# Second block's experts: token rows gathered as two halves to 128 partitions and turned in four transposes of 128

## The reference, cut to what matters

```python
# hier_moe_2: hf is (512, 1024); expert_idx (512, 2); weights (512, 2)
combine = jnp.sum(jax.nn.one_hot(expert_idx, 32) * weights[..., None], axis=1)
y = jnp.zeros_like(hf)
for e in range(32):
    he = jax.nn.silu(hf @ w_gate[e]) * (hf @ w_up[e])      # (512, 256)
    y = y + combine[:, e:e + 1] * (he @ w_down[e])         # (512, 1024)
```

## Time and profile before

| | us |
|---|---|
| median of 3 runs | 1526.12 |
| lowest and highest | 1524.87, 1528.68 |
| profiled execution: its own time | 1523.58 |
| its span (first to last instruction) | 1521.7 |

### The profile page before, as it was taken

The page is one execution under the profiler, slowest core; times in us unless marked ns, Lnnn a source line. Parts: engine busy times, 40 slices in busy tenths (PEclk is TensorE's granted clock), DMA queues, the critical chain, the costliest instruction groups (busy, mean ns, idle before and its releaser), DMA issues. The chain is left out here.

```text
span 1521.7 us, 20417 instructions
## 1 busy us (share of the span) xinstructions
PE 1296.7 (85%) x7696; PEld 1039.2 (68%) x7696; DVE 702.7 (46%) x1271; ACT 463.3 (30%) x1011; POOL 419.3 (28%) x358
## 2 busy tenths in 40 slices
PE   7997789949999259899999999999798939987882
PEld 6775567749999248789989888788676725544440
DVE  5787772644443556663745627571233341111112
ACT  4542343123232154442242422513323212111110
POOL 5355112111010214213414234134244112332212
PEclk9999889959999669999999999999899959999896
DMA  6300450179994603101213121222121879999994
GB/s 262 111 0 1 154 179 31 56 294 375 380 385 175 205 7 125 56 1 62 89 51 111 56 85 64 105 84 83 42 99 59 337 304 375 383 378 389 395 369 181
DMA packets 65286, 262.34 MB, mean 172 GB/s; under 512 B 8468, under 2 KB 18324, under 8 KB 52384
## 3 DMA queue, kind: packets, MB, share of 16 engines
q1 hardware_dynamic: 54176, 233.73, 41.0%
q0 software_dynamic: 9216, 20.99, 4.1%
q10 hardware_dynamic: 1792, 6.29, 1.2%
HBM read 242.04 MB, written 29.43 MB: 178 GB/s over the span
## 5 line engine op out<-in xcount | busy, mean ns | idle before, releaser
L1702 POOL TENSOR_TENSOR block_w_lo<-block_w,block_w_hi 128x512 fp32r<-128x512 f32 x96 | 130.5, 1361 | 221.2 <-ACT block_w_hi L1680 221.2
L2366 PE MATMUL e_gu<-e_w,e_xT 128*64 128x256 f32 x896 | 113.1, 410 | 22.8 <-DMA e_w<-in_gu 22.0
L240 PE MATMUL dil_bank<-block_w_hi,xT_hi 128*128 128x512 f32 x288 | 116.9, 406 | 4.3 <-PEq L829 4.3
L1680 ACT ACTIVATE block_w_hi<-block_w 128x512 fp32r<-128x512 f32 x96 | 60.7, 633 | 182.9 <-PE dil_bank L242 117.5
L241 PE MATMUL dil_bank<-block_w_lo,xT_hi 128*128 128x512 f32 x288 | 115.0, 399 | 0.0
L242 PE MATMUL dil_bank<-block_w_hi,xT_lo 128*128 128x512 f32 x288 | 114.9, 399 | 0.0
L2366 PEld LDWEIGHTS e_gu<-e_w,e_xT 128*64 128x64 f32 x896 | 67.4, 147 | 60.2 <-DMA e_w<-in_gu 24.5
L240 PEld LDWEIGHTS dil_bank<-block_w_hi,xT_hi 128*128 128x128 f32 x288 | 77.9, 271 | 8.7 <-issue 4.7
L2428 DVE TENSOR_TENSOR e_prod<-e_sg,e_gu 128x128 f32<-128x128 f32 x32 | 9.2, 289 | 156.0 <-ACT e_sg L2459 156.0
L241 PEld LDWEIGHTS dil_bank<-block_w_lo,xT_hi 128*128 128x128 f32 x288 | 78.1, 271 | 4.0
L242 PEld LDWEIGHTS dil_bank<-block_w_hi,xT_lo 128*128 128x128 f32 x288 | 77.8, 270 | 4.2
(11 more groups left out here) (505 smaller groups left out, 3150.5 us busy)
## 6 DMA issues: line engine op xcount, KB each, us to landing
e_w<-in_gu SPq DMA_DIRECT2D x44, 2048.0 KB, 18.1
e_w<-in_dn SPq DMA_DIRECT2D x48, 1024.0 KB, 20.0
block_w<-in_w_dil SPq DMA_DIRECT2D x9, 2048.0 KB, 8.2
block_w<-in_w_out SPq DMA_DIRECT2D x4, 2048.0 KB, 9.2
block_w<-in_w_gates SPq DMA_DIRECT2D x4, 2048.0 KB, 9.0
w_t<-in_w_in_t SPq DMA_DIRECT2D x12, 512.0 KB, 3.5
slot_rows<-blank SPq DMA_DIRECT2D x12, 512.0 KB, 6.7
slot_rows<-e_y ACTq DMA_DIRECT2D x16, 384.0 KB, 8.7
```

The lines of the kernel that those rows point to most:

```text
L240: pe.matmul(out, lhs[0], rhs[0], start=first, stop=False)
L1680: act.activation(wh[:, j % RING, 0:width[i]], k.w[:, slot, c, 0:width[i]], ACT.Copy).then_inc(hi_ready, 1)
L1702: pool.tensor_tensor(wl[:, j % RING, 0:width[i]], k.w[:, (q0 + i) % 2, c, 0:width[i]], wh[:, j % RING, 0:width[i]].bitcast(F32), ALU.subtr ...
L2366: ins = pe.matmul(gubank[t % 2][g * S:(g + 1) * S, 0:2 * FG], xT[t % 2][:, c * S:(c + 1) * S], w1_piece(slot.of[t], w, 2 * FG), start=(c = ...
```

## The change

`r_xg` is now 128 partitions by 512 in the second block. Partition p holds the first half of slot p's row, partition 64 + p its second half. The view `parts` sees `token_rows` as 1024 rows of 512 numbers, and `r_tok_of` grows to 128 partitions and holds twice the token plus 0 or 1. The new constant `row_half` (2048, or 2049 from partition 64 on) gives that in one DVE operation. A full 128 by 128 transpose of chunk c then turns features 128c to 128c + 127 of all slots, and, from the other partitions, features 512 + 128c on: four transposes in place of eight. `turned_at` says where a chunk now lies in `e_xbank` and `e_xT`. The first block's experts (96 slots) keep `GROUPS` = 1 and their whole rows.

```diff
-          ("half_row", 1), ("upto", 128), ...
+          ("half_row", 1), ("row_half", 1), ("upto", 128), ...
+    c["row_half"] = 2 * NO_TOKEN + k[:, None] // S2
...
-    k.tok_of = k.sb(ctx, f"{name}_tok_of", [S, NT], U32)
+    GROUPS = 2 if 2 * S == P else 1
+    k.tok_of = k.sb(ctx, f"{name}_tok_of", [GROUPS * S, NT], U32)
+    parts = rows.rearrange("t (m f) -> (t m) f", m=GROUPS)
+    k.xg = [k.sb(ctx, f"{name}_xg{i}", [GROUPS * S, DM // GROUPS]) for i in range(2)]
...
-    k.xg = [k.sb(ctx, f"{name}_xg{i}", [S, DM]) for i in range(2)]
...
-                    pool.indirect_dma_start(k.xg[b][:], None, rows, bass.IndirectOffsetOnAxis(
-                        ap=k.tok_of[:, b:b + 1], axis=0), bounds_check=SEQ - 1, oob_is_err=False).then_inc(x_in[b], 16)
+                    pool.indirect_dma_start(k.xg[b][:], None, parts, bass.IndirectOffsetOnAxis(
+                        ap=k.tok_of[:, b:b + 1], axis=0), bounds_check=GROUPS * SEQ - 1, oob_is_err=False).then_inc(x_in[b], 16)
...
-                dve.tensor_scalar(k.tok_of[:], tbank[0:S, 0:NT], float(NO_TOKEN), None, ALU.add).then_inc(tok_ready, 1)
+                if GROUPS == 1:
+                    ins = dve.tensor_scalar(k.tok_of[:], tbank[0:S, 0:NT], float(NO_TOKEN), None, ALU.add)
+                else:
+                    ins = dve.tensor_scalar(k.tok_of[:], tbank[:, 0:NT], float(GROUPS), k.c("row_half"), ALU.mult, ALU.add)
+                ins.then_inc(tok_ready, 1)
...
+        parts = rows.rearrange("t (m f) -> (t m) f", m=GROUPS)
+        PER = KD // GROUPS
+
+        def turned_at(c):
+            return (c % PER * GROUPS + c // PER) * S
...
-                    for c in range(KD):
-                        ins = pe.transpose(xbank[c * 2 // KD][:, c * S % XH:c * S % XH + S],
-                                           xg[t % 2][:, c * P:(c + 1) * P], k.c("ident")[0:S, 0:S])
+                    for c in range(PER):
+                        at = turned_at(c)
+                        ins = pe.transpose(xbank[at // XH][:, at % XH:at % XH + U], xg[t % 2][:, c * P:(c + 1) * P],
+                                           k.c("ident"))
...
-                            ins = pe.matmul(gubank[t % 2][g * S:(g + 1) * S, 0:2 * FG], xT[t % 2][:, c * S:(c + 1) * S],
+                            ins = pe.matmul(gubank[t % 2][g * S:(g + 1) * S, 0:2 * FG], xT[t % 2][:, turned_at(c):turned_at(c) + S],
                                             w1_piece(slot.of[t], w, 2 * FG), start=(c == 0), stop=(c == KD - 1))
```

More of the change, by code:

```diff
@@ L74 @@
 CONSTS = [("ident", 128), ("before", 128), ("ones", 128), ("iota", 128), ("down", 128), ("tok", TT), ("freq", 16),
-          ("half_row", 1), ("upto", 128), ("after", 128), ("rot", 128), ("cos", SEQ), ("sin", SEQ)]
+          ("half_row", 1), ("row_half", 1), ("upto", 128), ("after", 128), ("rot", 128), ("cos", SEQ), ("sin", SEQ)]
 CONST_AT = {}
@@ L2326, in tile @@
                         pool.wait_ge(x_turned, t - 1)
-                        pool.indirect_dma_start(xg[t % 2][:], None, rows, bass.IndirectOffsetOnAxis(
-                            ap=k.tok_of[:, t:t + 1], axis=0), bounds_check=SEQ - 1, oob_is_err=False).then_inc(
+                        pool.indirect_dma_start(xg[t % 2][:], None, parts, bass.IndirectOffsetOnAxis(
+                            ap=k.tok_of[:, t:t + 1], axis=0), bounds_check=GROUPS * SEQ - 1, oob_is_err=False).then_inc(
                                 x_in[t % 2], 16)
```

## The result

The changed kernel took 1508.41 us (median of 1505.68, 1506.26 and 1510.56), the kernel before beside it 1525.89 us. The ratio is 0.9876, with a 95% interval of 0.9855 to 0.9896: **17.5 us, 1.2%, faster**. A fourth run of the changed kernel took 2619.2 us, in a slow state that no other run showed, and is left out. The prediction had 1526.0 us, a range from 1522.0 to 1529.5, and a chance of 0.04 for this side.

What follows compares the result with a forecast made beforehand. The prediction took the second block's expert stage to be DMA-bound. Its terms, 0.05 + 0.12 + 0 + 0 - 0.22 + 0, summed to -0.05 us, giving 1526.0 us for the median, range 1522.0 to 1529.5.

Steps and rivals of the forecast that it cites:

- What bounds the kernel: Second block's experts: DMA engines stay busy and set the stage's end; loads from 1333 us on wait in their queue.
- DMA time of the stream: Second block's stream: gathers hold the engines about 11.6 us and half rows are no dearer; 0 us, range -3.6 to +3.6.
- the good end: Gathers in the stream: if 257 GB/s is the price of 64 partitions, 30 gathers fall from 15.2 to 11.6 us, -3.6 us.
- spreading over 128 partitions helps: Faster rival: first landings gain 2.5 us and the stream's gathers 3.6 us, together -6.1 us, 1519.9 us; chance 0.04.
- Token numbers: Stage's start: the operation on 128 partitions takes 0.25 us instead of 0.20 on 64; +0.05 us on the path.
- Issues of gathers: POOL at the stage's start: 1014 ns per gather instead of 953, two on the path; +0.12 us.
- Packets: First two gathers: two half rows share a packet, so 80 packets per gather and 160 for two, as before.
- half rows cost more: Slower rival: reading 2 KB pieces at half the present rate makes gathers take 23.2 us, not 11.6; 1537.6 us; chance 0.05.
- First landings: First two gathers, before the drain where the engines meet: landing unchanged, 0 us, range -2.5 to +2.5.
- Turn of tile 0: PE at the stage's start, clock 0.50: four transposes of 128 take 1.11 us, eight of 64 took 1.10; 0 us.
- Turn at full clock: PE, tiles 1 and 2: four transposes take 0.60 us instead of 0.71, -0.22 us on the path; other 29 turns hidden.
- Later landings: Gathers issued two tiles ahead, 9.8 us before need: landing stays as it is and PE does not wait; 0 us.

Runs made afterwards that it cites:

- the padded kernel: Kernel before with second-block gathers over 128 partitions, indices of partitions 64 to 127 out of bounds, whole rows on the same 64 partitions: 1517.7 us, ratio 0.9944.
- after_again: The changed kernel itself, unchanged, in a later comparison: 1508.51 us (6 runs) against 1525.65 us for the kernel before, ratio 0.989.

## Why the prediction was wrong

What bounds the kernel: **right**. The DMA engines are the bound from 1333 us on. That is why a change of the rate came through in full: 16.4 us from the stream's first regular load to its last landing, 17.9 us in the span.

The step that failed is **"DMA time of the stream"**. I asked how many microseconds the gathers hold the engines, 11.6, took the good end as 257 GB/s turned into 337, and got at most 3.6 us. Two things were wrong in it. First, the term held only q0's own packets. It took q1's 387 GB/s as a constant, though the question of the change was what a transfer does to the loads beside it. q0's own part was 2.4 us for gathers and scatters together, within the bounds; q1's was 14.2 us, and had no term at all. Second, the row was there. The earlier trace rows shows 257 GB/s while 64-partition gathers moved their rows, and I put it down to "the end of other loads". That reading was wrong: in this microsecond (1244:1245, first fence) q1 had 7.3% of the engines' time. In the same one of the changed kernel (second fence) the first gathers moved their rows at 0.21 / 0.579 = 363 GB/s.

```profile
q1 hardware_dynamic: 16, 0.02, 7.3%
```

```profile
q0 software_dynamic: 121, 0.21, 57.9%
```

The right use of the row would have been to look at the same moment in the dense part. The windows of 1 us above have it in the trace of before: 303 to 365 GB/s when a gather's rows move, 393 to 475 between. A shortfall of some 100 GB/s over 2 to 3 us is 0.2 to 0.3 MB, at 420 GB/s 0.5 to 0.7 us of stream per gather, and 30 gathers make 14 to 21 us. That estimate could have been made blind.

The same view would have given a ceiling: a DMA share of 1.01 is busy time, not speed. Between gathers the same queues moved up to 475 GB/s; the mean of 387 left something to be found.

The rival **"spreading over 128 partitions helps"** had the direction, at 1519.9 us and 0.04. Its mechanism was sized by the same wrong term.

The Trainium skill, "SBUF — State Buffer", section "Can I just issue two DMAs to hit both halves?", says that the ports of the on-chip memory that a transfer uses go by its own span of partitions, and that only one transfer over all 128 reaches all 16. The cut gather agrees with it in its time: two gathers over 64, one to each half, gave 1528.56 us where one over 128 gave 1508.51 us. I had instead weighed what the Trainium skill, "DMA: Bandwidth & Descriptors", section "Rules for kernel authors", says of tile shapes, that 128 partitions mean more and smaller descriptors, and had taken it to speak against the change; 1728 further packets of skipped rows did not raise q0's share (9.9%). The price falls on q1's loads above all, as their packets show. The Trainium skill, "DMA: Bandwidth & Descriptors", section "The descriptor swizzle", gives for 128 partitions which engine writes which partitions, the first eight engines the lower 64. The late end of the padded kernel (1481.45 us, share down to 0.31) fits rows on eight engines only. That 64-partition rows are written by engines whose loads go elsewhere, through ports that others' loads need, is my reading of all this. It fits the scatter, which reads on-chip memory and hinders nothing, and it is argued, not shown: no run separated the port from other consequences of the dealing, and the traces name neither a packet's engine nor its port. What is shown ends at the instruction: over 64 partitions it makes the loads' packets beside it longer, over 128 it does not.

The other steps. Token numbers: 0.27 us, expected 0.25. Issues of gathers: 1.07 and 1.01 us, expected 1.01 each. Packets: two gathers make 160 packets and 0.24 MB, as predicted, so "half rows cost more" fell as expected. First landings: the drain ended 1.1 us earlier, within -2.5 to +2.5 us. Turn of tile 0: 1.11 us, as predicted. Turn at full clock: 0.66 us in the timeline at 1253.51 against 0.71, and the chain's tile is 6.33 us long (1258.40 to 1264.73) instead of the 6.27 predicted: 0.05 us gained a tile, not 0.11, since the price came from a group of four transposes elsewhere. Not in the sum was that gate and up of tile 0 ran 0.77 us shorter. The mean granted clock of that stretch was 0.74 (1248.6 to 1253.6) instead of 0.63 (1249.7 to 1255.4): both begin at the lower level (0.50, 1.2 GHz), and it rose sooner. That is an accident of the execution and no effect of the change: in another profile of the changed kernel (after_again) the same products took 6.16 us, and the first regular load went out at 1254.49. Later landings: 8.0 us in the median and 9.2 at most for the stage's 30 gathers, and no wait for `r_xg` on the chain: right.

## What to carry over

When a kernel is bound by a stream of transfers, read its GB/s in windows of a microsecond, not only its DMA share: a share of 1.0 at 315 GB/s beside 475 a few microseconds later is a transfer that is being hindered, and a small one beside it may be the reason. Price an edit of a transfer by what it does to the queue that carries the bytes, not by its own packets alone. In a stage like this one, let an indirect gather that runs beside large loads be one instruction over 128 partitions with its rows spread over all of them, by halving the rows or even by skipped indices; where TensorE was the bound, in the first block, it brought nothing (1510.58 us).

## What was new of the hardware

- A gather of 64 partitions costs the loads of another queue more than it takes itself: 30 gathers whose own packets hold the engines for an estimated 11.6 us cost the kernel 27 to 30 us. Over 128 partitions the cost is 12 to 13 us (all known to some 7 us). In a stage with the first kind 30.1% of the loads' 16 KB packets took over 650 ns, with the second 0.7%.
- Two gathers over 64 partitions to the two halves of the memory are no substitute for one over 128: 1528.56 against 1508.51 us.
- The direction matters: the scatter, from on-chip memory to HBM, cut the same way cost nothing measurable (1509.8 us).
- Skipped rows took no measurable time of the engines: 5888 packets instead of 4160 on q0 at a share of 9.9 against 10.5%. But where all valid rows lie in the lower 64 of 128 partitions, the time was 9.2 us longer than the changed kernel's; with the same rows spread over both halves 6.7 of them were gone.
